# Second attention of a two-layer stream step: where VectorE makes the decode weights and where TensorE transposes the prompt weights

## The reference

```python
def stick_breaking_attention(q, k, v, q_pos0):
    ...
        z = jnp.einsum('bqhd,bkhd->bhqk', qb, kb).astype(jnp.float32) * scale
        q_pos = q_pos0 + jnp.arange(start, stop)
        mask = jnp.arange(k_end)[None, :] < q_pos[:, None]
        log_1m = jnp.where(mask, jax.nn.log_sigmoid(-z), 0.0)
        suffix = lax.cumsum(log_1m, axis=3, reverse=True) - log_1m
        a = jnp.where(mask, jnp.exp(jax.nn.log_sigmoid(z) + suffix), 0.0)
        outs.append(jnp.einsum('bhqk,bkhd->bqhd', a.astype(v.dtype), vb))
    ...
```

## Time and profile before

| | before |
|---|---|
| median of 3 runs | 1647.85 us (1647.73 to 1648.43) |
| the profiled execution, its own time | 1649.32 us |
| its span in the profile | 1647.5 us |
| TensorE matmul busy | 1616.3 us, 98% |
| VectorE busy | 1151.9 us, 70% |
| ScalarE busy | 740.6 us, 45% |
| second attention, first decode transpose of slot 0 to the first output-projection matmul | 998.64 to 1158.14 |

### The profile page before, as it was taken

The page is one execution under the profiler, slowest core; times in us unless marked ns, Lnnn a source line. Parts: engine busy times, 40 slices in busy tenths (PEclk is TensorE's granted clock), DMA queues, the critical chain, the costliest instruction groups (busy, mean ns, idle before and its releaser), DMA issues.

```text
span 1647.5 us, 31458 instructions
## 1 busy us (share of the span) xinstructions
PE 1616.3 (98%) x13140; PEld 1483.3 (90%) x13140; DVE 1151.9 (70%) x1605; ACT 740.6 (45%) x1228; POOL 145.7 (9%) x123
## 2 busy tenths in 40 slices
PE   8999999999999999999999999999999999999999
PEld 6888766699999999999999896666999999999999
DVE  5765477668984797488742328989689848974874
ACT  5444366765541344134432215768555413531441
POOL 0000000012210011012000000000122201110110
PEclk9999999999999999999999999999999999999999
DMA  7133899941222122222244358996412221221222
GB/s 286 52 111 132 350 418 418 419 160 52 86 94 103 52 78 103 77 78 78 103 166 140 112 209 360 420 418 288 167 66 89 95 85 52 103 102 53 78 103 90
DMA packets 39596, 265.45 MB, mean 161 GB/s; under 512 B 4256, under 2 KB 4640, under 8 KB 10272
## 3 DMA queue, kind: packets, MB, share of 16 engines
q1 hardware_dynamic: 36720, 252.95, 39.8%
q0 software_dynamic: 2736, 10.49, 1.8%
HBM read 247.69 MB, written 15.73 MB: 160 GB/s over the span
## 4 chain that ended last, share of the span: by engine, by line
PE 85%; DVE 8%; DMA 3%; issue 2%; ACT 2%; SPq 0%; DVEq 0%; ACTq 0%
PE ps L584 30%; PE ps L799 28%; PE ps L268 5%; PE ps L269 4%; PE ps L270 4%; PE ps L1260 2%; PE ps L1319 2%; DVE s_lo L748 2%; PE ps L611 2%; PE ps L1204 2%; DMA kv<-in_v_a 1%; PE ps L1238 1%; DMA xT<-in_v_a 1%; PE ps L1225 1%; DVE pw L1621 1%
## 5 line engine op out<-in xcount | busy, mean ns | idle before, releaser
L230 ACT ACTIVATE w_hi<-w_raw 128x2048 fp32r<-128x2048 f32 x55 | 105.1, 1910 | 190.3 <-PE ps L584 158.5
L246 DVE TENSOR_TENSOR w_lo<-w_raw,w_hi 128x2048 fp32r<-128x2048 f32 x55 | 126.0, 2291 | 71.4 <-ACT w_hi L230 71.4
L744 ACT ACTIVATE s_hi<-t 128x512 fp32r<-128x512 f32 x176 | 109.4, 626 | 144.6 <-PE ps L799 65.8
L799 PE MATMUL ps<-hs_hi,s_hi 128*128 128x320 f32 x528 | 163.8, 310 | 0.0
L799 PE MATMUL ps<-hs_hi,s_lo 128*128 128x320 f32 x528 | 163.2, 309 | 0.0
L799 PE MATMUL ps<-hs_lo,s_hi 128*128 128x320 f32 x528 | 163.1, 309 | 0.0
L584 PE MATMUL ps<-gu_hi,w_hi 128*128 128x320 f32 x692 | 157.9, 309 | 0.2
L584 PE MATMUL ps<-gu_lo,w_hi 128*128 128x320 f32 x692 | 157.7, 309 | 0.0
L584 PE MATMUL ps<-gu_hi,w_lo 128*128 128x320 f32 x692 | 157.6, 309 | 0.0
L748 DVE TENSOR_TENSOR s_lo<-t,s_hi 128x512 fp32r<-128x512 f32 x176 | 132.8, 760 | 5.4 <-ACT s_hi L744 4.6
L268 PE MATMUL ps<-w_hi,h_hi 128*128 128x512 f32 x320 | 126.8, 396 | 8.1 <-DVE h_lo L300 8.1
(11 more groups left out here) (298 smaller groups left out, 3995.9 us busy)
## 6 DMA issues: line engine op xcount, KB each, us to landing
w_raw<-in_w SPq DMA_DIRECT2D x99, 1024.0 KB, 4.8
kv<-in_k_a SPq DMA_DIRECT2D x12, 1024.0 KB, 16.1
kv<-in_v_a SPq DMA_DIRECT2D x12, 1024.0 KB, 16.7
kv<-in_v_s SPq DMA_DIRECT2D x12, 1024.0 KB, 12.6
kv<-in_k_s SPq DMA_DIRECT2D x12, 1024.0 KB, 15.0
xT<-in_k_a SPq DMA_DIRECT2D x8, 1024.0 KB, 17.4
xT<-in_k_s SPq DMA_DIRECT2D x8, 1024.0 KB, 11.7
work<-in_v_a SPq DMA_DIRECT2D x7, 1024.0 KB, 14.9
```

The costliest lines, as they stand in the source:

```text
L230: nc.scalar.activation(w_hi[s][:, :, :], w_raw[:, s, :, :], ACT.Copy).then_inc(hi_done, 1)
L246: nc.vector.tensor_tensor(w_lo[s][:, :, :], w_raw[:, s, :, :], w_hi[s][:, :, :].bitcast(F32), ALU.subtract).then_inc(lo_done, 1)
L744: nc.scalar.activation(s_hi[i][:, :, :], factor(j % 2, i), ACT.Copy).then_inc(hi_done, 1)
L799: last = nc.tensor.matmul(ps[:, bank[i], 0:HALF], w[:, p, :], m[:, p, :], start=(i < 3 and p == 0 and a == 0), stop=(p == 3 and a == 2), s ...
```

## The change

Two edits, both in the second attention. On VectorE, `dve_sprod(n + 1)` (the next pair's decode weights) is issued ahead of `dve_prod(k + 2)` (the weights of the next prompt step), in every slot. On TensorE, `rounds` holds the transpose rounds of the slot; it has three entries in every slot but the first. In even slots (from 2 on) they are the two rounds of step k-1 (i = 3) and the one of step k (i = 0), in odd slots the one round of step k-1 (i = 1) and the two of step k (i = 2). Before, two rounds stood ahead of the decode transposes in every slot. Now two stand there in even slots and one in odd slots, so the first round of step k moves behind the decode transposes in odd slots. Nothing is added or left out, ScalarE's list and SyncE's queue are unchanged.

```diff
@@ -1377,17 +1377,18 @@
                 for n in range(N_PAIRS):
                     k = 2 * n
                     rounds = self.slot_rounds(n)
+                    ahead = 1 + (n + 1) % 2
                     self.pe_ps(k + 1)
                     if n % 2 == 1:
                         self.pe_pv(k - 2)
-                    for j, r in rounds[:2]:
+                    for j, r in rounds[:ahead]:
                         self.pe_pt(j, r)
                     self.pe_w1(n)
                     self.pe_w2(n)
                     self.pe_wn(n)
                     if n > 0:
                         self.pe_o(n - 1)
-                    for j, r in rounds[2:]:
+                    for j, r in rounds[ahead:]:
                         self.pe_pt(j, r)
                     if n + 1 < N_PAIRS:
                         self.pe_ps(k + 2)
@@ -1786,10 +1787,10 @@
                     self.dve_prod(ch, k + 1, lambda: self.dve_new(n))
                     if n % 2 == 0 and n + 2 < N_PAIRS:
                         self.dve_q(n // 2 + 1)
+                    if n + 1 < N_PAIRS:
+                        self.dve_sprod(ch, n + 1)
                     if k + 2 < STEPS:
                         self.dve_prod(ch, k + 2)
-                    if n + 1 < N_PAIRS:
-                        self.dve_sprod(ch, n + 1)
```

## The result

| | before | change |
|---|---|---|
| median (6 runs each) | 1648.10 us | 1661.41 us (1660.43 to 1663.09) |
| ratio of the change to before | | 1.0082, 95% interval 1.0072 to 1.0093 |
| the profiled execution, its own time | 1649.32 us | 1663.09 us |
| its span | 1647.5 us | 1661.3 us |
| second attention, slot 0's first decode transpose to the projection | 159.50 us | 173.66 us |

Slower by 13.3 us; forecast were 9.8, with a range that ends 0.1 us above what was measured. The profiled execution of the change is the slowest of its six: 13.8 us over the profiled one of before, and its second attention 14.2 us longer. All of the loss lies there: from the first projection matmul to the end of the span it takes 489.4 us before and 489.5 after.

What follows compares the result with a forecast made beforehand. VectorE was taken to set the pace, TensorE just behind. Start +1.92, six pairs at 21.03 us (9.19 + 11.84) with a 1.40 pause +6.30, end +1.54: +9.8 us, median 1657.6, range 1652.0 to 1661.5.

Steps and rivals of the forecast that it cites:

- the even stretch: From L1283's start in an even slot to the end of the odd slot's decode weights: forecast 9.19 us.
- W: Start of L1283, TensorE's decode transposes, in an even slot; forecast pairs of these starts 21.03 us apart against 19.30.
- O: End of VectorE's decode weights for the odd slot, forecast 9.19 us after the even slot's L1283 start.
- the two pauses of even slots: TensorE pauses after even slots' scores, 1.36 and 1.38 us, forecast to fall into new idle time and cost nothing.
- VectorE idle in even slots: VectorE waits for ScalarE's sigmoid(-z) before the decode scan, about 2.3 us, in place of 384-column work.
- The odd stretch: From the end of the odd slot's decode weights to the next even slot's L1283: forecast 11.84 us.
- The wait of the moved transposes: TensorE in odd slots idles 1.5 us before the four moved transposes, for VectorE's 384-column product.
- the one at L1269: TensorE in odd slots waits for swn and the stores; without it a pair would be 0.33 us shorter.
- The clock: Rival, 3%: new 1.5 us idle drops TensorE to 1.2 GHz, at most +9.6 us per slot, 1667 with one.
- The pauses: Four unexplained TensorE pauses, 5.38 us in all, kept in place; odd-slot 1.24 and 1.40 on the path; fetches left undecided.
- faster: Rival, 3%: decode weights come first, so TensorE's waits for them and the moved transposes go; 1641.8 us at best.
- no change: Rival, 6%: VectorE's lost 2.3 us is slack, since pauses kept it waiting anyway; 1648 to 1650 us.

Runs made afterwards that it cites:

- Experiment 5: The full change, but scans of step k+2 ahead of the decode scan, only their product behind the decode weights: 1649.21 us, ratio 1.0000 to before.
- experiment 3: The full change, but VectorE's decode weights first in even slots alone, behind the 128-column step in odd slots: 1661.41 us, ratio 1.0089 to before.
- experiment 4: The full change, but VectorE's decode weights first in odd slots alone, behind the 384-column step in even slots: 1650.24 us, ratio 1.0016 to before.
- experiment 6: The full change, but in odd slots VectorE stores swn and the last output ahead of the 512-column scans: 1658.28 us, ratio 1.0058 to before.
- Experiment 7: The full change, but in even slots ScalarE copies the first round ahead of sigmoid(z) of step k+1: 1658.75 us, ratio 1.0060 to before.
- Experiment 2: The change with VectorE's new order alone, TensorE's transposes placed as in the kernel before: 1668.82 us, ratio 1.0138 to before.
- experiment 9: The full change plus stores ahead of the 512-column scans (odd slots) and first-round copy ahead of sigmoid(z) (even slots): 1653.45 us, ratio 1.0040 to before.
- experiment 8: The full change plus ten identity transposes into a free PSUM bank ahead of the moved transposes in odd slots: 1664.14 us, ratio 1.0091 to before.
- experiment 11: The full change plus scans ahead of the decode scan, stores ahead of 512-column scans (odd slots), copy ahead of sigmoid(z) (even slots): 1644.23 us, ratio 0.9982 to before.

## Why the prediction came out too low

The path was right: each wait that it named is there. The step that failed is a term of the sum, the even stretch: 9.19 us were taken from W to O, and it takes 9.57. A fall of the clock, left out of the sum, adds 1.2 us in the profile. That the range still holds the result, by 0.1 us, is luck: its upper end stands for the two pauses of even slots lying on the path too (+2.7), and one of them fell into idle time and the other was not there. The even starts by pair, in us:

| slots | before | forecast | change |
|---|---|---|---|
| 0 to 2 | 19.99 | 21.91 | 21.09 |
| 2 to 4 | 19.80 | 21.03 | 21.51 |
| 4 to 6 | 20.86 | 21.03 | 22.04 |
| 6 to 8 | 20.71 | 22.43 | 23.88 |
| 8 to 10 | 21.31 | 21.03 | 22.13 |
| 10 to 12 | 19.32 | 21.03 | 21.40 |
| 12 to 14 | 19.28 | 21.03 | 21.40 |
| 14 to the projection | 18.23 | 19.77 | 20.21 |
| sum | 159.50 | 169.26 | 173.66 |

**VectorE idle in even slots**: forecast 2.3 us, measured 2.0 to 2.7. Experiment 5 fills it, and the loss is gone; experiments 3 and 4 place it in the even slots. Right.

**The odd stretch**: forecast 11.84 us from the end of the decode weights to the next L1283. In the change, from 1028.80 (1027.56 + 1.24) to 1040.76: 11.96, and 11.83 to 11.85 in slots 9, 11 and 13. The wait of the moved transposes (forecast 1.5, and 1.4 to 1.6 as the sign; measured 1.35) and the one at L1269 (0.33 and 0.32) are there, and experiment 6 shows the second on the path. Right.

**The even stretch, the term that failed**: I took W + 4.51 us for the start of sigmoid(-z) from slot 4. In that slot TensorE had waited 0.37 us at L1283, and in that time ScalarE had done sigmoid(z) and the copy of the first round. In the change TensorE arrives last, the copy is 0.22 us late for it, and the way is 4.89. O is W + 9.57 (1130.21 to 1138.54 + 1.24), not 9.19: 0.38 us in each of the seven even slots from 2 on, 2.7 of the 4.4 us by which the stage's forecast was short. The trace of before had it: in slots 2 and 8 TensorE did not wait at L1283 and waited 0.23 us for the copy, and the way there is 4.89 as well (1018.63 to 1023.52; TensorE's row, then ScalarE's):

```profile
1020.12 0.41 PE L1225 MATMUL ps<-const,pp 128*128 128x128 f32 x2 [0.23 <-ACT wt L1439]
```

```profile
1023.52 1.04 ACT L1460 ACTIVATE sw<-ps 128x1040 f32<-128x1040 f32 x1 [0.39 <-PE ps L1273]
```

Experiment 7 takes the copy out of the way and gets 4.46 us and 0.44 a pair back. What to learn from it: a distance read behind a wait is too short for a kernel in which the wait is gone.

**The clock** was given 3% as a rival of its own; the path is the one forecast, and one fall comes on top of it. TensorE's clock in three neighbouring windows of the change, columns as in the earlier trace rows:

```profile
1084.00:1086.00 2.00, 0.90 (x7) 0.86 (x8) 1.13 (x5) 0.60 (x1) 0.00 (x0) 0.90 0.96 401
1086.00:1088.00 2.00, 2.00 (x12) 2.00 (x11) 1.25 (x2) 1.02 (x3) 0.00 (x0) 0.50 1.06 446
1088.00:1090.00 2.00, 2.00 (x13) 1.46 (x13) 0.80 (x4) 1.92 (x5) 0.00 (x0) 0.74 0.83 340
```

It is at its lower level, 1.2 GHz, for most of the time from 1085.6 to 1089, behind this pause, after a stretch in which TensorE waited 1.36 and 0.32 us already:

```profile
1085.10 0.20 PE L1210 MATMUL ps<-steps 64*128 64x64 bf16 x2 [1.68 <-issue]
```

In that stretch eight prompt transposes take 1.45 us from start to the next group (0.93 elsewhere), and L1283 to L1204 2.55 (1.83 elsewhere): 1.2 us. Experiment 2, with waits of 2.05 to 3.47 us in one piece, has the fall in four of seven pairs, at 1.6 us each. Experiments 3, 6 and 9 have seven falls behind the waits of 1.35 to 1.40 us that the change made, so the condition of that rival (idle time of 1.5 us) can bring a fall; behind most such waits the clock stayed. The Trainium skill (TensorE: Matmul & The Clock Gate, HAM oscillation) tells of a clock that falls in every turn of a loop, in waits of 3 to 5 us for DMA. Here the trace agrees in part: shorter waits than those brought falls, and the same wait of 2.45 us was followed by a fall in some pairs and not in others. My price for a fall, 9.6 us a slot, was far too high: it lasted a third of a slot and cost 1.2 us.

**The pauses**: 1.37 us in slot 4 fell into the idle time as forecast; the first after slot 1's scores was 0.35 and not 1.24 (0.9 less), the one of slot 7 1.68 and not 1.40. The slots 4 to 6 have 1.0 more than forecast: 0.38 is the copy, 0.5 lies in slot 5 in the value products between L1269 and L1238, a new pause of 0.26 among them, and 0.1 is the odd stretch, as in slot 3. The question that the prediction left open, whether such pauses are fetches of instructions, the traces answer with yes as far as their timing can tell (last section); and they did not all stay, as it took them to.

**The rivals**: faster and no change are out. Their common ground, that VectorE's lost time might be slack, falls with experiments 3 and 5.

## What to carry to other kernels

In a strict queue, moving the urgent work first helps only if its input is there: otherwise the queue waits with it, and the work that used to fill the wait comes out late behind it. Split the filler if only part of it fits (scans ahead, product behind). And when a distance between two engines is read from a trace, look whether the first had waited just before: its helpers used that wait, and without it the distance is longer.

## What the runs showed of the hardware

- TensorE's granted clock fell to 1.2 GHz 15 times in the second attentions of the 14 profiles: four times in experiment 2 (waits of 2.25 to 3.47 us in one piece), seven times in experiments 3, 6 and 9 (waits of 1.35 to 1.40 us), and four times at pauses of 1.68 to 1.91 us (the change, experiments 4 and 5). It stayed at 2.4 GHz behind waits of 2.05 to 2.45 us in experiment 2, a pause of 2.13 us in experiment 8, and pauses of 1.40 us before. So the length of the last idle time alone does not decide it. Where the rest of a pair is undisturbed, a fall made it 0.6 to 1.6 us longer. The kernel before is not free of falls either: none is in its profile, but its run of 1652.55 us has a mean granted clock of 0.996.
- TensorE's pauses that no wait ends (0.2 to 2.1 us) sum to 6.47 us in before's profile, 4.7 in the change, 1.67 in experiment 11, 0.86 in experiment 9. Runs of one kernel differ by 4 us and more (before: 1643.42 to 1652.55 over all runs of this study), about what the pauses sum to. That the pauses are the difference between such runs was not tried.
- The traces do show where the pauses belong. Beside the loads, one DMA queue carries packets of the kind "instruction", 16384 bytes each; the page of before has it as (packets, MB, share of the DMA engines):

```profile
q8 instruction: 105, 1.72, 0.4%
```

  TensorE has 13140 matmuls and as many weight loads, 250 for each of the 105 packets. Experiment 8, which gives TensorE more instructions, has 106. Some 20 such packets pass in the second attention. In the 14 profiles every one of the 49 pauses of 0.2 us or more ends 1.21 to 1.59 us behind the end of one: in before a packet ends at 1045.55 and the pause of slot 4 at 1046.90, in the change at 1048.14 and 1049.60. The pauses also stand mostly at the same few instructions from kernel to kernel (L1327 in slot 1, L1238 in slot 4, L1319 in slot 5 or 8, L1210 in slot 7) and move when experiment 8 puts ten instructions more into each odd slot. So they are TensorE waiting for its own next instructions; this is read from the traces, no run changed the fetches by themselves. The Trainium skill (Runtime: NRT & Kernel Launch, Instruction fetch mechanics) calls an engine's fetch of instructions mostly hidden; the traces agree for most packets (15 of 20 in before's second attention pass without a pause), and the others stop TensorE for up to 2.1 us each. What makes one come late, and what made them rare in experiments 9 and 11, is open.
